# A decoder layer's recurrent branch: sigmoids and gelu through tanh, convolution from an SBUF tile

## What is computed

```
h = rmsnorm(x, g_mix);  proj = h @ w_in          # [q | k | v | lx | lg], lx and lg 512 wide
attn = sliding_window_attention(rope(q), rope(k), v, sinks)      # window 128
lx = causal_depthwise_conv(lx, conv_w, conv_b)   # 4 taps over positions
r = sigmoid(lx_blocks @ w_a + b_a);  i = sigmoid(lx_blocks @ w_x + b_x)
log_a = -8 * r * softplus(-lam);  a = exp(log_a)
h_t = a * h_(t-1) + sqrt(1 - a^2) * i * lx       # associative scan over positions
lru = h_t * gelu(lg)                             # tanh form of gelu
x = x + concat(rmsnorm(attn), rmsnorm(lru)) @ w_out
x = x + hierarchical_moe(rmsnorm(x))             # 4 groups x 8 experts, top-1 group, top-2 experts
x = x + sigmoid(rmsnorm(x) @ w_ple_gate) * (p @ w_ple_proj)
out = rmsnorm(x, g_final)
```

## Time and profile before

| | us |
|---|---|
| median of 3 runs | 1473.58 (1471.18 to 1474.04) |
| profiled execution, its own time | 1483.52 |
| its span (slowest core, core 0) | 1481.9 |
| spans of the eight cores | 1437.9 to 1481.9 |
| prefix blocks (end about) | 180 |
| own blocks (end about) | 592 |
| dispatch (end about) | 650 |

### The profile page before, as it was taken

The page is one execution under the profiler, slowest core; times in us unless marked ns, Lnnn a source line. Parts: engine busy times, 40 slices in busy tenths (PEclk is TensorE's granted clock), DMA queues, the critical chain, the costliest instruction groups (busy, mean ns, idle before and its releaser), DMA issues.

```text
span 1481.9 us, 24750 instructions; the slowest of 8 cores (1437.9 to 1481.9 us)
## 1 busy us (share of the span) xinstructions
PE 1117.1 (75%) x7772; PEld 718.8 (49%) x7772; DVE 731.3 (49%) x1283; ACT 728.3 (49%) x1376; POOL 489.2 (33%) x576
## 2 busy tenths in 40 slices
PE   2546679989989887047789979989698896942882
PEld 1212235555555545035566757667476665621431
DVE  4899886777768964741122212212121121117993
ACT  4898987877867973012233333323233232313652
POOL 3222222322213332023243424434333452211673
PEclk9766757867769988558899989999899998975996
DMA  9999996763605923309999999999879899478422
GB/s 237 214 174 110 109 109 100 150 93 102 120 8 86 149 95 122 147 21 194 182 222 206 178 207 211 205 206 203 195 159 215 191 188 180 135 233 323 148 114 115
DMA packets 71967, 235.44 MB, mean 159 GB/s; under 512 B 23447, under 2 KB 30359, under 8 KB 55712
## 3 DMA queue, kind: packets, MB, share of 16 engines
q0 software_dynamic: 43984, 134.60, 55.3%
q1 hardware_dynamic: 27856, 99.25, 19.9%
HBM read 415.98 MB, written 101.71 MB: 349 GB/s over the span
## 4 chain that ended last, share of the span: by engine, by line
PE 46%; DMA 20%; DVE 10%; issue 10%; ACT 7%; POOL 4%; SPq 1%; DVEq 0%; ACTq 0%; POOLq 0%
PE ps L1377 14%; DMA sb_R<-h2scr,sb_R 12%; PE ps L1349 8%; PE ps L966 4%; DMA sb_R<-w_pp 3%; PE ps L750 2%; PE ps L840 2%; PE ps L1003 2%; PE ps L1332 2%; DMA sb_R<-xin 1%; PE ps L902 1%; DMA sb_R<-yscr 1%; DMA sb_R<-wall,sb_R 1%; PE ps L1517 1%; PE ps L903 1%
## 5 line engine op out<-in xcount | busy, mean ns | idle before, releaser
L1377 PE MATMUL ps<-sb_R 128*128 128x256 bf16 x3008 | 346.9, 277 | 6.6 <-DMA sb_R<-wall,sb_R 4.9
L1377 PEld LDWEIGHTS ps<-sb_R 128*128 128x128 bf16 x3008 | 297.9, 99 | 56.7 <-issue 8.1
L1359 POOL DMA_INDIRECT yscr<-sb_R x94 | 94.6, 1007 | 364.1 <-DVE sb_R L1356 345.6
L1382 DVE TENSOR_TENSOR sb_R<-sb_R,ps 128x512 bf16<-128x512 f32 x94 | 64.7, 688 | 301.8 <-PE ps L1377 271.0
L1335 ACT COPY sb_R<-ps 128x1024 bf16<-128x1024 bf16 x94 | 95.1, 1012 | 190.4 <-PE ps L1332 184.6
L1349 PE MATMUL ps<-sb_R 128*128 128x512 bf16 x752 | 184.9, 401 | 0.8 <-DVE sb_R L1356 0.2
L1356 DVE COPY sb_R<-ps 128x512 f32<-128x512 f32 x94 | 65.0, 692 | 232.4 <-PE ps L1349 149.7
L1381 ACT ACTIVATE sb_R<-ps 128x512 f32<-128x512 f32 x94 | 56.1, 597 | 228.7 <-PE ps L1377 228.6
L1303 POOL DMA_INDIRECT sb_R<-h2scr,sb_R x94 | 97.7, 1039 | 92.1 <-DVE sb_R L1262 63.6
L1349 PEld LDWEIGHTS ps<-sb_R 128*128 128x128 bf16 x752 | 74.9, 103 | 90.8 <-issue 22.7
L1332 PE MATMUL ps<-sb_id,sb_R 128*128 128x128 bf16 x752 | 57.8, 236 | 64.3 <-DMA sb_R<-h2scr,sb_R 63.8
(11 more groups left out here) (247 smaller groups left out, 2104.9 us busy)
## 6 DMA issues: line engine op xcount, KB each, us to landing
sb_R<-wall POOLq DMA_DIRECT2D x66, 1024.0 KB, 22.4
wbf<-wall POOLq DMA_DIRECT2D x30, 1024.0 KB, 43.9
sb_R<-wbf SPq DMA_DIRECT2D x30, 1024.0 KB, 12.5
sb_R<-xin SPq DMA_DIRECT2D x32, 512.0 KB, 18.8
sb_R<-yscr SPq DMA_DIRECT2D x16, 1024.0 KB, 6.7
xscr<-sb_R SPq DMA_DIRECT2D x16, 512.0 KB, 3.7
sb_R<-xscr SPq DMA_DIRECT2D x16, 512.0 KB, 12.8
out<-sb_R SPq DMA_DIRECT2D x16, 512.0 KB, 2.7
```

Source lines behind the costliest of these rows:

```text
L1359: return e.indirect_dma_start(y_d, bass.IndirectOffsetOnAxis(ap=didx[:, blk:blk + 1], axis=0), y.ap, None, bounds_check=breg(e, 2 * T_OWN ...
L1377: ins = e.matmul(pv[:, q * N:(q + 1) * N], lhsT=w_[:, c, f * P:(f + 1) * P], rhs=hT_[:, c, 0:N], start=(c == 0), stop=(c == 7))
L1382: S.op("dve", lambda e: e.tensor_tensor(hid[s % 2][:, fp * 2:fp * 2 + 2, 0:N], sgs[fp][:, 0:2 * N].rearrange("p (q t) -> p q t", q=2), pu. ...
```

## The change

Line numbers of the changed kernel are some 3 to 6 off those of before. Five things change:

- **Sigmoids.** sigmoid(z) = (1 + tanh(z/2))/2. Two tanh on the gates (L774, L775), the affine part folded into the scale and bias of the two following exps (L776, L777; a pointer for each), one ln (L778), one exp with the half folded in as a bias of ln 0.5 (L779). 1 + tanh is applied on VectorE (L780), which takes the place of L783. ACT has six 128x512 activations for nine.
- **Gelu.** One tanh (L802) for exp, ln, exp; the factor 2 is taken out in the norm (L805, L819).
- **Convolution.** ACT copies `pl` into a tile `lx` of 516 columns (L759), in front of which POOL has put the three carried columns (L758); VectorE forms all four taps from `lx` over the full 512 positions (L760, L762 three times), and POOL stores the last three columns (L765). L763 and L766 are gone.
- **Rings.** `LX` has 4 buffers; `F10` has 12 for 14.
- **Scheduler.** Tanh counts as belonging to exp's table, ln to another, and exp to either. A change of table now puts 20 on the priority of the candidate in place of 1.4 us on its start, and 1.3 us on its time once picked.

```diff
@@ -15,6 +15,8 @@
 HOP = 0.22
 ALPHA = 0.1
 AHEAD = 700
+SWITCH = 20.0
+SETS = {AF.Exp: ("exp", "ln"), AF.Ln: ("ln",), AF.Tanh: ("exp",), AF.Silu: ("silu",), AF.Sigmoid: ("sig",), AF.Sin: ("sin",)}
 
...
@@ -86,10 +88,8 @@
 
     def activation(self, out, in_, func, bias=None, scale=None, accum_out=None):
         self.c += 0.2 + fsize(in_) * 0.00083 + (0.2 if accum_out is not None else 0.0)
-        if func in (AF.Exp, AF.Ln):
-            self.table = "el"
-        elif func in (AF.Silu, AF.Sigmoid, AF.Sin):
-            self.table = func
+        if func in SETS:
+            self.table = SETS[func]
         return self
 
     def copy(self, out, in_):
@@ -355,9 +355,8 @@
                         if v.pool.free:
                             r = max(r, min(v.pool.ftime[i] for i in v.pool.free))
                     st = max(t, r)
-                    if e == "act" and o.table is not None and o.table != table:
-                        st += 1.4
-                    cand.append((st, -o.prio + ALPHA * o.idx, o.idx, o))
+                    sw = e == "act" and o.table is not None and table not in o.table
+                    cand.append((st, -o.prio + ALPHA * o.idx + (SWITCH if sw else 0.0), o.idx, o))
...
@@ -389,8 +388,9 @@
-            if o.eng == "act" and o.table is not None:
-                table = o.table
+            if o.eng == "act" and o.table is not None and table not in o.table:
+                table = o.table[0]
+                st += 1.3
             fin = st + o.cost
             tz[o.eng] = fin
             if o.dma:
...
@@ -639,7 +640,8 @@
...
-        F10 = R.pool(S, "f1024", 1024, 14)
+        F10 = R.pool(S, "f1024", 1024, 12)
+        LX = R.pool(S, "lx", 516, 4)
...
@@ -698,13 +701,13 @@
-        S.op("dve", lambda e: e.tensor_scalar(der[:, :, 0], der[:, :, 5], -8.0, None, ALU.mult),
+        S.op("dve", lambda e: e.tensor_scalar(der[:, :, 0], der[:, :, 5], -4.0, None, ALU.mult),
-        S.op("dve", lambda e: e.tensor_scalar(der[:, :, 1], der[:, :, 5], -16.0, None, ALU.mult),
+        S.op("dve", lambda e: e.tensor_scalar(der[:, :, 1], der[:, :, 5], -8.0, None, ALU.mult),
-        S.op("dve", lambda e: e.tensor_scalar(der[:, :, 2], colp[:, :, 5], -1.0, None, ALU.mult),
+        S.op("dve", lambda e: e.tensor_scalar(der[:, :, 2], colp[:, :, 5], 0.5, None, ALU.mult),
...
@@ -751,19 +754,15 @@
                                    rhs=hv()[:, c, :], start=(c == 0), stop=(c == 7))
                 return ins
             S.op("pe", mm, reads=[WinL_b if cc < 2 else WinL2_b, hT], writes=[pl])
-            S.op("dve", lambda e: e.tensor_scalar(cv.ap, pl.ap, colp[:, cc, 3:4], colp[:, cc, 4:5], ALU.mult, ALU.add),
-                 reads=[pl, colp_b], writes=[cv])
+            lx = S.v(LX)
+            S.op("pool", lambda e: e.tensor_copy(lx[:, 0:3], carry[:, cc, 0:3]), reads=[carry_b[cc]], writes=[lx])
+            S.op("act", lambda e: e.copy(lx[:, 3:515], pl.ap), reads=[pl], writes=[lx])
+            S.op("dve", lambda e: e.tensor_scalar(cv.ap, lx[:, 3:515], colp[:, cc, 3:4], colp[:, cc, 4:5], ALU.mult, ALU.add), reads=[lx, colp_b], writes=[cv])
             for j in range(2, -1, -1):
-                sh = 3 - j
-                S.op("dve", lambda e, j=j, sh=sh: e.scalar_tensor_tensor(
-                    cv[:, sh:512], pl[:, 0:512 - sh], colp[:, cc, j:j + 1], cv[:, sh:512], ALU.mult, ALU.add),
-                    reads=[pl, colp_b, cv], writes=[cv])
-            if blk > 0:
-                for j in range(3):
-                    S.op("dve", lambda e, j=j: e.scalar_tensor_tensor(
-                        cv[:, 0:3 - j], carry[:, cc, j:3], colp[:, cc, j:j + 1], cv[:, 0:3 - j], ALU.mult, ALU.add),
-                        reads=[carry_b[cc], colp_b, cv], writes=[cv])
-            S.op("dve", lambda e: e.tensor_copy(carry[:, cc, 0:3], pl[:, 509:512]), reads=[pl], writes=[carry_b[cc]])
+                S.op("dve", lambda e, j=j: e.scalar_tensor_tensor(
+                    cv.ap, lx[:, j:j + 512], colp[:, cc, j:j + 1], cv.ap, ALU.mult, ALU.add),
+                    reads=[lx, colp_b, cv], writes=[cv])
+            S.op("pool", lambda e: e.tensor_copy(carry[:, cc, 0:3], lx[:, 512:515]), reads=[lx], writes=[carry_b[cc]])
             S.op("pool", lambda e: e.tensor_copy(cvb.ap, cv.ap), reads=[cv], writes=[cvb])
             pga = psv(); pgx = psv()
             S.op("pe", lambda e: e.matmul(pga.ap, lhsT=wabd[:, cc, :], rhs=cvb.ap, start=True, stop=True),
@@ -772,17 +771,14 @@
                  reads=[wbd_b, cvb], writes=[pgx])
             t0 = S.v(F5); t4 = S.v(F5); t2 = S.v(F5); t3 = S.v(F5)
             A = AF
-            S.op("act", lambda e: e.activation(t0.ap, pga.ap, A.Exp, scale=-1.0, bias=der[:, cc, 2:3]), reads=[pga, der_b], writes=[t0])
-            S.op("act", lambda e: e.activation(t4.ap, pgx.ap, A.Exp, scale=-1.0, bias=der[:, cc, 3:4]), reads=[pgx, der_b], writes=[t4])
-            S.op("act", lambda e: e.activation(t0.ap, t0.ap, A.Ln, bias=1.0), reads=[t0], writes=[t0])
-            S.op("act", lambda e: e.activation(t0.ap, t0.ap, A.Exp, scale=-1.0), reads=[t0], writes=[t0])
-            S.op("act", lambda e: e.activation(t2.ap, t0.ap, A.Exp, scale=der[:, cc, 0:1]), reads=[t0, der_b], writes=[t2])
-            S.op("act", lambda e: e.activation(t3.ap, t0.ap, A.Exp, scale=der[:, cc, 1:2]), reads=[t0, der_b], writes=[t3])
+            S.op("act", lambda e: e.activation(t0.ap, pga.ap, A.Tanh, scale=0.5, bias=der[:, cc, 2:3]), reads=[pga, der_b], writes=[t0])
+            S.op("act", lambda e: e.activation(t4.ap, pgx.ap, A.Tanh, scale=0.5, bias=der[:, cc, 3:4]), reads=[pgx, der_b], writes=[t4])
+            S.op("act", lambda e: e.activation(t3.ap, t0.ap, A.Exp, scale=der[:, cc, 1:2], bias=der[:, cc, 1:2]), reads=[t0, der_b], writes=[t3])
+            S.op("act", lambda e: e.activation(t2.ap, t0.ap, A.Exp, scale=der[:, cc, 0:1], bias=der[:, cc, 0:1]), reads=[t0, der_b], writes=[t2])
             S.op("act", lambda e: e.activation(t3.ap, t3.ap, A.Ln, scale=-1.0, bias=1.0), reads=[t3], writes=[t3])
-            S.op("act", lambda e: e.activation(t4.ap, t4.ap, A.Ln, bias=1.0), reads=[t4], writes=[t4])
-            S.op("dve", lambda e: e.scalar_tensor_tensor(t3.ap, t3.ap, 0.5, t4.ap, ALU.mult, ALU.subtract), reads=[t3, t4], writes=[t3])
-            S.op("act", lambda e: e.activation(t3.ap, t3.ap, A.Exp), reads=[t3], writes=[t3])
-            S.op("dve", lambda e: e.tensor_tensor(t3.ap, t3.ap, cv.ap, ALU.mult), reads=[t3, cv], writes=[t3])
+            S.op("act", lambda e: e.activation(t3.ap, t3.ap, A.Exp, scale=0.5, bias=lnh_ap), reads=[t3, eps_b], writes=[t3])
+            S.op("dve", lambda e: e.scalar_tensor_tensor(t4.ap, t4.ap, 1.0, cv.ap, ALU.add, ALU.mult), reads=[t4, cv], writes=[t4])
+            S.op("dve", lambda e: e.tensor_tensor(t3.ap, t3.ap, t4.ap, ALU.mult), reads=[t3, t4], writes=[t3])
...
@@ -803,12 +799,10 @@
             S.op("pe", mm2, reads=[WinG_b, hT], writes=[plg])
             S.op("act", lambda e: e.activation(t6.ap, plg.ap, A.Square, scale=GELU_S), reads=[plg], writes=[t6])
             S.op("dve", lambda e: e.scalar_tensor_tensor(t6.ap, t6.ap, 1.0, plg.ap, ALU.add, ALU.mult), reads=[t6, plg], writes=[t6])
-            S.op("act", lambda e: e.activation(t6.ap, t6.ap, A.Exp, scale=-GELU_C), reads=[t6], writes=[t6])
-            S.op("act", lambda e: e.activation(t6.ap, t6.ap, A.Ln, bias=1.0), reads=[t6], writes=[t6])
-            S.op("act", lambda e: e.activation(t6.ap, t6.ap, A.Exp, scale=-1.0), reads=[t6], writes=[t6])
+            S.op("act", lambda e: e.activation(t6.ap, t6.ap, A.Tanh, scale=0.5 * GELU_C), reads=[t6], writes=[t6])
             S.op("dve", lambda e: e.tensor_tensor(t5.ap, plg.ap, hl.ap, ALU.mult), reads=[plg, hl], writes=[t5])
-            S.op("dve", lambda e: e.tensor_tensor(t5.ap, t5.ap, t6.ap, ALU.mult), reads=[t5, t6], writes=[t5])
-            S.op("act", lambda e: e.activation(sq.ap, t5.ap, A.Square), reads=[t5], writes=[sq])
+            S.op("dve", lambda e: e.scalar_tensor_tensor(t5.ap, t6.ap, 1.0, t5.ap, ALU.add, ALU.mult), reads=[t5, t6], writes=[t5])
+            S.op("act", lambda e: e.activation(sq.ap, t5.ap, A.Square, scale=0.5), reads=[t5], writes=[sq])
             S.op("pool", lambda e: e.tensor_copy(yT.ap, t5.ap), reads=[t5], writes=[yT])
             return yT, sq
 
@@ -822,7 +816,7 @@
                 return ins
             S.op("pe", mmss, reads=sqs + [ones128_b], writes=[pss])
             S.op("act", lambda e: e.activation(rbc.ap, pss.ap, AF.Ln, scale=1.0 / 512.0, bias=eps_ap), reads=[pss, eps_b], writes=[rbc])
-            S.op("act", lambda e: e.activation(rbc.ap, rbc.ap, AF.Exp, scale=-0.5), reads=[rbc], writes=[rbc])
+            S.op("act", lambda e: e.activation(rbc.ap, rbc.ap, AF.Exp, scale=-0.5, bias=lnh_ap), reads=[rbc, eps_b], writes=[rbc])
             for cc in range(4):
                 S.op("dve", lambda e, cc=cc: e.tensor_tensor(yTs[cc].ap, yTs[cc].ap, rbc.ap, ALU.mult),
```

8 lines of the change are left out of this document (5 added, 3 removed).

## The result

| | before | changed |
|---|---|---|
| median, us | 1473.0 | 1497.4 (1495.9 to 1499.5) |
| ratio | | 1.0168, 95% interval 1.015 to 1.0185 |
| profiled execution: span of the slowest core, us | 1481.9 | 1495.2 |

What follows compares the result with a forecast made beforehand. DVE and ACT alternating were taken to bound the prefix, PE the own blocks. Prefix -7, own blocks -3 and elsewhere 0 made -10 us, from 1473.6 to 1463.6 us, range 1446 to 1484.

Steps and rivals of the forecast that it cites:

- `F10` with 12 buffers delays x loads that are three blocks ahead: nothing: Ring of 1024-word tiles: two buffers fewer would only delay x loads three blocks ahead, at no cost.
- table loads: ACT before 592 us: 27 more loads of 1.4 us, +38 us, against 47.0 us of activations saved.
- the decay exps: ACT, each chunk: two exps gain one more pointer each and already have one, so no cost.
- the taps: DVE's convolution: three taps reading SBUF cost +0.03 us each, +0.09 per chunk.
- tap 3: DVE's convolution: this tap reads SBUF and takes 0.45 us, so -0.27 us per chunk.
- the drain: ACT's table switches: the skill's about 1380 ns beside each load; the row showed none of that size.
- Prefix -7: 48 to 180 us: DVE -10 and ACT -5.4 alternate on the path, so -7 us, between the two.
- DVE's -10: Prefix, 48 to 180 us: DVE loses 10 us from -0.62 us per chunk.
- Nothing behind 592 us: Dispatch and experts: untouched by the change, 0 us; earlier gains or losses reach the end whole.
- The own blocks' -3: 222 to 592 us: ACT loses 3.8 and DVE 10, PE sets the pace, so only -3 us arrives.
- ACT is held up: Rival, chance 0.18: ACT's list waits on other-table runs, loads and POOL at L759; +10 us, range +4 to +20.
- Its term for the loads, +14: Own blocks, in the held-up rival: 20 loads of 1.4 us, 28 us, half of them delaying PE, +14 us.

Runs made afterwards that it cites:

- without loads: Changed kernel with 14 `F10` buffers, `lx` from the 640-word ring, and Exp run in place of Tanh; ratio 0.9956 to the kernel before.
- the three cuts: Rings of 512, 256 and 128 words one buffer smaller each: 0.9999 in the kernel before; 1.0205 in the changed kernel with 14 `F10` and 2 `lx` buffers.

## Why the prediction was wrong, step by step

- **"`F10` with 12 buffers delays x loads that are three blocks ahead: nothing"** is the step that failed. Measured: 11 us in the kernel before, 17 in the changed one, 16 in the version for the prefix only, each with the list that the scheduler makes for the ring. It is not the delay of an x load as such: on core 5 the 28th starts 4 us later than before and lands 3 us earlier. I had counted the x loads that are far ahead and not the loads and router tiles of the next block, which draw on the same ring; whichever of them stands first in ACT's list without a buffer or its data (an x square in the change, the router's copy in the kernel before with 12) turns that into idle time of ACT, DVE and PE. The clock adds to it: PE came back from the pause at 0.51, and of the own blocks' loss on cores 4 to 7 some 11 us are longer busy time of PE at 0.83 for 0.86.
- Without it the change is still 0.37% slower (5 us), not 10 faster. That remainder goes with the **table loads**. Their number was right (34 loads of 1283 ns), as was their length of 1.4 us with the start lost (the earlier trace rows shows one load, not the two that the prediction speaks of). Booked were 38 us against 47 saved, as ACT time that mostly disappears in slack. They cost some 12 us of the end, while the 47 us of saved activations and DVE's savings brought together 6 (0.9956 without loads). In the prefix ACT was to lose 5.4 us and is busy 122.1 instead of 115.4 (48 to 180 us, means): on core 5, 13 loads stand there for 3, where 7 more were booked, and 12 squares of x for 8, work of later tiles.
- ACT's other terms: the copy L759 starts 0.47 us before its follower (275.71 to 276.18), for 0.52 booked; the decay exps, booked at nothing for their second pointer, take 820 and 814 ns for 714 and 722 and start 0.72 us apart for 0.61, some 7 us over 64. I had not priced it. To the router mark ACT's busy time fell by 6.5 us, booked 9.
- DVE: the taps 784 ns for 740, maximum 1529, so +0.04 for +0.03; tap 3 575 for 805, so -0.23 for -0.27. DVE's sum to the router mark fell by 15.3 us, booked 20. These steps held. On core 5 the 39 taps that ran beside no POOL instruction took 746 ns, at most 753, and the 57 others 806, up to 1529. This is the rule of the Trainium skill ("SBUF — State Buffer", Practical consequences), and it was a small term. The Trainium skill there excepts the 2-port modes from its sentence on one SBUF input, which the prediction left out; tap 3, with one such input, took at most 548 ns alone and up to 1291 beside POOL.
- Of the drain that the Trainium skill ("ScalarE: Activation LUTs", What ACT_TABLE_LOAD costs) puts beside a load nothing is seen: the 13 loads at L778 above have 0.2 us of idle time before them in all, and L774 starts 0.02 us behind its load. 33 loads cost 12 us of the end, where 2.66 us each would be 88 of ACT.
- POOL: 13 us booked for the small copies, they take 28, and the casts went from 732 to 919 ns; busy in 48 to 180 us 58.8 for 24.5 on core 5. No wait of ACT at L759 for POOL came of it, as forecast.
- Prefix -7: the prefix mark moved by -9, but the last chunk of block 3 by -2 only, so the number came out nearly right for a stretch that reaches into block 4, and blocks 0 to 3 gained less than forecast. DVE's -10 there was -1.5 in busy time (48 to 180 us, means, with work of later blocks in it). Nothing behind 592 us: 2 us, which held. The own blocks' -3 was +30, on cores 4 to 7 +37. There I read PE as the pace from the earlier trace rows, where core 0 was unlike the others: at a granted clock of 0.80 it was busy 333.9 of 370 us, core 5 at 0.85 only 309.2 of the same 370. Mean PE idle of before from 48 us to the router mark is 110 us, and this grew.
- The rival with the right sign, *ACT is held up*, had ACT held by runs of the other table and by POOL. ACT was held up, but in the main by a DMA, and its +10 was too small. Its term for the loads, +14, is near the 12 measured. Its sign, PE waiting over 15 us for tanh lines, did show (15.3 us at L774), though through the stall.

What stays open: why the kernel with 2 `lx` buffers and the three cuts is slow, and why either part alone is slower than both with as many buffers (convolution 1.0278 against 1.0168 with 12, tanhs 1.013 against 1.0037 with 14). The new table rule of the scheduler was never run by itself. Each edit makes the scheduler write a new list, and these lists differ by 10 to 20 us in PE's busy and idle time without a wait that explains it. That the DMAs of the precast make the x loads of this stretch slow (22.8 us, before 30.7) is read from the DMA share only; a kernel with the precast moved wasn't tried, and without them the short ring might cost less.

## What to carry to other kernels

Before a ring of tiles is cut, list all that draw on it and find the tightest moment; here 12 buffers for 14 cost 11 to 17 us, mostly as one wait of an in-order engine for a buffer or its data. What a chain of activations saves on an engine with slack is worth much less than its busy time, and so is a load of tables in the same chains (a quarter of its time here). Before a mark is read as the end of a stage, see that both lists have the same work in front of it. Where one stretch gains and another loses, apply the change to the first alone: here blocks 0 to 3 gave 0.3% with the ring kept and 0.5% with one buffer more, where the whole lost 1.7%.

## Unexpected of the hardware

An activation with scale and bias both from pointers took 820 and 814 ns, the same two with one pointer 714 and 722. A POOL copy of 128x3 took 550 ns (L758) and 368 ns (L765), where a cast of 128x512 took 919. But on core 5 the eight L758 that ran beside no DVE instruction took 220 ns on average, the 24 others 611; that the rest is waiting for DVE is a reading, no run tests it. A 512 KB load issued under a DMA share of 0.99 landed after 22.8 us in the change and the same load of before after 30.7, while the three issued some 5 us ahead of it there took 5 to 14.
